# A hybrid decoder layer on one core: gate's low-rank product spread over the first projection, one warm-up matmul less, decay levels in pairs

## The chip, the cores and the metric

The kernel runs on one core of a Trainium2 chip. The metric is the device time of one execution in microseconds, from repeated executions. The profile is of one further execution; its engines are TensorE (PE, with the weight loads PEld apart), VectorE (DVE), ScalarE (ACT), GpSimd (POOL) and SyncE (SP), which issues nearly all DMAs.

## The reference

One layer on 256 tokens of width 1024, all in float32:

```python
def _hybrid_mixer(h, w_in, w_gate_up, b_gate, gla_norm_g, w_mix_o):
    proj = h @ w_in
    qa, ka, va, qg, kg, vg, rg, glr = jnp.split(proj, cuts, axis=-1)
    moba_o = _merge(_moba(_heads(qa, 8), _heads(ka, 8), _heads(va, 8)))
    log_a = jax.nn.log_sigmoid(glr @ w_gate_up + b_gate) / GLA_GATE_TEMP
    o = _gla(_heads(qg, 4), _heads(kg, 4), _heads(vg, 4), _heads(log_a, 4))
    o = o * lax.rsqrt(jnp.mean(jnp.square(o), -1, keepdims=True) + RMS_EPS) * gla_norm_g
    gla_o = _merge(o) * jax.nn.silu(rg)
    return jnp.concatenate([moba_o, gla_o], -1) @ w_mix_o

def reference(...):
    x = _layer_norm(ALPHA * x + _hybrid_mixer(x, ...), ln1_g, ln1_b)
    x = _layer_norm(ALPHA * x + _mem_xattn(x, mem, w_xq, w_xkv, w_xo), ln2_g, ln2_b)
    return _layer_norm(ALPHA * x + jnp.square(relu(x @ w_ff1)) @ w_ff2, ln3_g, ln3_b)
```

Group A is causal softmax attention (8 heads of 64), group B gated linear attention (4 heads, key width 64, value width 128, chunks of 64 tokens). Its gate comes from a low-rank product: glr has 16 columns, w_gate_up is 16x256. Within a chunk the attention of t to s is the sum over d of q[t,d] k[s,d] exp(b[t,d] - b[s,d]), with b the running sum of log_a.

## The kernel before, in words

**Precision.** A float32 operand is split into a high part (fp32r, a rounded copy made by ScalarE) and a low part (operand minus high part, by VectorE, for a few units by POOL). A projection is three products of such parts: high times high, high times low, low times high. Products of attention (scores, transposes, decay levels) run in plain float32. For the first projections the helpers `high` and `low` (L1371 and L1377 on) make it two: the high weights meet both parts of the input in one matmul of 512 columns (L1374), the low weights the high input in one of 256 (L1378).

**Weights** come in chunks of 512 columns or rows (2 MB), each in two halves of 1 MB ("units"), through a ring of four buffers, `raw`. SyncE issues a load once the low part of the unit four places earlier is made. ScalarE's `hi_half(c, half)` casts a unit into `w_hi`, VectorE's `lo_half(c, half)` subtracts into `w_lo`; both of these have two places, by the chunk's parity, so ScalarE may start on a chunk once TensorE is through with the one two before. Chunk 0 is gate queries and keys (qg, kg), 1 queries (qa), 2 keys (ka), 3 values (va), 4 and 5 values and the output gate of group B (vg, rg), 6, 7, 8, 11 the memory's keys and values, 9 and 10 the output projection.

**The first chunk** is cut finer: input and weights land alternately in eight DMAs, and `EARLY_CUTS` lists the nine pieces in which ScalarE (L564) and VectorE (L878) split them. Behind these, `w_glr` (the 16 columns of the low-rank product, 64 KB) is loaded (L378) and split into `wglr_split` (L567, L881).

**Order of work.** Every engine's order is written out by hand. PSUM has eight banks; `FRONT_FILLS` lists which product fills which bank, in order, and `begin(name)` waits until the bank's earlier content has left, `full(name)` tells that it is filled, `wait_out(name)` waits until it has been copied out. TensorE does, in this order: `WARM_UP` = 3 matmuls of 512 columns on constants (L1366; the profile shows each as two pieces); chunk 0, for each k of eight four high and four low matmuls; the low-rank product glr, 16 matmuls (L1402, L1403); half of the queries; z = glr times w_gate_up (L1426); the other half; the keys ka0 to ka3, one after another, each eight high matmuls and then eight low ones; va, scores, vg, and so on.

**Decay levels.** The attention within chunks is made in seven levels (blocks of 64, 32, ... 1) and one product across chunks (`off`). For each level VectorE makes exponents, ScalarE the exponential, POOL the products with keys and queries (L478, L488), TensorE four float32 matmuls (L1501; eight pieces in the profile), and VectorE copies what belongs to the level under a mask (`masked`, L1006). POOL's product for level n waits until TensorE has done level n - 2. The levels stand between the memory's projections xk0 to xk3, xv00, xv01, one after each half of a projection.

**DVE's order at the keys** is: low part of chunk 2's first half, z plus bias (L911), its absolute value (L916), low part of the second half (L869).

Of the kernel before, what the change touches and what calls it, by code (L numbers as in the profile page):

```python
# [21 lines left out]
S = 256  # L22
# [4 lines left out]
RANK = 16  # L27
# [11 lines left out]
WARM_UP = 3  # L39
# [71 lines left out]
def raw_count(u):  # L111
# [5 lines left out]
    [("qg0", 0), ("qg1", 1), ("kg0", 2), ("kg1", 3), ("glr", 4), ("qa0", 5), ("qa1", 6), ("qa2", 7), ("qa3", 0), ("z", 4),  # L117
     ("ka0", 1), ("ka1", 2), ("ka2", 3), ("ka3", 4), ("va0", 2)]
# [23 lines left out]
def build(nc, x, xT, memT, w_in, w_glr, w_gate_up, b_gate, gla_norm_g, w_mix_o, ln1_g, ln1_b, w_xq, w_xkv,  # L142
# [7 lines left out]
    with ctx:  # L150
# [200 lines left out]
        def _(sp):  # L351
# [176 lines left out]
        def _(act):  # L528
# [36 lines left out]
            act.wait_ge(wglr_in, 16)  # L565
            act.wait_ge(wglr_zeroed, 1)
            act.copy(wglr_parts[:, :, 0:3, 0, :], wglr_thrice).then_inc(wglr_hi, 1)  # L567
# [3 lines left out]
            hi_half(1, 0)  # L571
            right("qg0")
# [3 lines left out]
            wait_full(act, "glr")  # L576
            act.copy(glrT[:], bank[4][0:6 * RANK, 0:S]).then_inc(glr_hi, 1)
# [99 lines left out]
            memk(3)  # L677
            decay(7)
# [4 lines left out]
            hi_half(9, 0)  # L683
# [174 lines left out]
        def _(dve):  # L858
# [17 lines left out]
            for n, (u, _, a, b) in enumerate(EARLY_CUTS):  # L876
# [3 lines left out]
            dve.wait_ge(wglr_hi, 1)  # L880
            dve.tensor_tensor(wglr_parts[:, :, 0:3, 1, :], wglr_thrice, wglr_parts[:, :, 0:3, 0, :].bitcast(f32),  # L881
                              ALU.subtract).then_inc(wglr_lo, 1)
            def left(name):
# [7 lines left out]

            lo_half(1, 0)
# [6 lines left out]
            low_rows = slice(2 * RANK, 4 * RANK)  # L899
            b = wait_full(dve, "glr")  # L900
            dve.wait_ge(glr_hi, 1)
            dve.tensor_tensor(glrT[low_rows, :], b[low_rows, 0:S], glrT[low_rows, :].bitcast(f32), ALU.subtract)\
                .then_inc(freed("glr"), 1)
# [18 lines left out]
            lo_half(3, 0)  # L922
            for m in range(4):
                left(f"qa{m}")
            lo_half(3, 1)
# [116 lines left out]
            masked(0)  # L1042
            exponents(4)
            masked(1)
            lo_half(8, 0)
            exponents(5)
            masked(2)
            lo_half(8, 1)
            exponents(6)
            masked(3)  # L1050
            exponents(7)
            masked(4)
            masked(5)
            masked(6)
            lo_half(9, 0)
# [231 lines left out]
        def _(pe):  # L1287
# [93 lines left out]

            first = ["qg0", "qg1", "kg0", "kg1"]
            banks = [begin(name) for name in first]
            for k in range(8):
                unit_w, end = 1 + k // 4, 512 * (k % 4) + 512
                if k >= 2:
                    end = 1024 * (k % 4 // 2) + 1024
                if k < 2 or k % 2 == 0:
                    pe.wait_ge(early_lo, early_count(0, 512 * (k // 2) + 512))
# [9 lines left out]
            b = begin("glr")  # L1399
            pe.wait_ge(wglr_lo, 1)  # L1400
            for k in range(8):
                pe.matmul(b[:, 0:S], wglr_split[:, k, :], actA_hi[:, k, :], start=k == 0, stop=False)  # L1402
# [311 lines left out]
```

## Time and profile before

| | us |
|---|---|
| median of 3 runs | 411.12 |
| lowest, highest | 410.32, 411.77 |
| the profiled execution, its own time | 409.76 |
| its span | 407.9 |
| TensorE busy | 400.2 (98%) |
| VectorE, ScalarE, GpSimd busy | 278.1, 204.3, 63.7 |

The span is from the first to the last instruction on the core; the execution's own time has some more around it. Busy shares say which engine works most. What sets the end is told by the chain that ended last: it is followed back from the last instruction, at each step to what released it. TensorE's ends are modelled, since its matmuls are pipelined.

### The profile page before, as it was taken

What the parts mean: (1) busy time and instruction counts of PE and PEld (TensorE: products, weight loads), DVE (VectorE), ACT (ScalarE), POOL (GpSimd) and SP (SyncE); (2) the same over time, 40 slices, a digit from 0 to 9 for tenths busy, and PEclk for the clock granted to TensorE, in tenths of its full rate; (3) what the DMA queues carried; (4) which work ended last, traced back from release to release, by engine and by line L of the source; (5) the groups of instructions that cost most, each with busy time, mean ns of one, the idle gap of its engine ahead of it and who ended that gap; (6) DMA issues with size and microseconds to landing.
All of it is one profiled execution on the core that took longest, in us unless ns stands there. A gap on an engine that the chain in (4) does not pass through costs nothing.

```text
span 407.9 us, 5836 instructions
## 1 busy us (share of the span) xinstructions
PE 400.2 (98%) x2256; PEld 345.9 (85%) x2256; DVE 278.1 (68%) x357; ACT 204.3 (50%) x279; POOL 63.7 (16%) x61
## 2 busy tenths in 40 slices
PE   8999999999999999999999999999999999999993
PEld 5888888899988888999988888888888888888882
DVE  3679676998794796876658859384746475664826
ACT  5658478646354628435833457362625343545400
POOL 2089000045960105000005100000000000000000
PEclk9999999999999999999999999999999999999999
DMA  8998737635535380733554284656665727464002
GB/s 288 318 372 283 245 136 268 225 128 207 182 128 206 105 306 3 274 141 104 206 196 158 73 297 127 204 186 206 208 206 169 242 104 257 153 217 194 0 0 103
DMA packets 32220, 75.70 MB, mean 186 GB/s; under 512 B 1510, under 2 KB 3910, under 8 KB 32198
## 3 DMA queue, kind: packets, MB, share of 16 engines
q1 hardware_dynamic: 31808, 75.24, 53.4%
q10 hardware_dynamic: 390, 0.17, 0.2%
q8 instruction: 14, 0.23, 0.2%
q14 instruction: 8, 0.07, 0.0%
HBM read 74.35 MB, written 1.05 MB: 185 GB/s over the span
## 4 chain that ended last, share of the span: by engine, by line
PE 98%; DVE 1%; issue 0%; POOL 0%; DVEq 0%; POOLq 0%
PE bank L1300 21%; PE bank L1301 21%; PE bank L1302 21%; PE bank L1653 13%; PE bank L1656 7%; PE bank L1374 5%; PE bank L1378 3%; PE bank L1501 2%; PE bank L1366 1%; PE bank L1306 1%; PE bank L1453 1%; PE bank L1479 0%; PE bank L1534 0%; PE bank L1583 0%; PE bank L1445 0%; PE bank L1444 0%
## 5 line engine op out<-in xcount | busy, mean ns | idle before, releaser
L869 DVE TENSOR_TENSOR w_lo<-raw,w_hi 128x2048 fp32r<-128x2048 f32 x36 | 83.7, 2330 | 20.0 <-ACT w_hi L539 20.0
L539 ACT CAST w_hi<-raw 128x2048 fp32r<-128x2048 f32 x38 | 72.3, 1916 | 20.1 <-PE bank L1302 14.2
L1235 DVE TENSOR_TENSOR w_lo<-raw,w_hi 128x2048 fp32r<-128x2048 f32 x24 | 55.0, 2291 | 40.1 <-ACT w_hi L806 40.1
L1300 PE MATMUL bank<-w_hi,actB_hi 128*128 128x512 f32 x192 | 75.6, 394 | 0.0
L1301 PE MATMUL bank<-w_lo,actB_hi 128*128 128x512 f32 x192 | 74.8, 390 | 0.0
L1302 PE MATMUL bank<-w_hi,actB_lo 128*128 128x512 f32 x192 | 74.8, 389 | 0.0
L806 ACT CAST w_hi<-raw 128x2048 fp32r<-128x2048 f32 x24 | 46.0, 1917 | 38.2 <-PE bank L1302 38.2
L1653 PE MATMUL bank<-actA,w_hi 128*128 128x512 f32 x224 | 56.0, 392 | 0.0
L1653 PEld LDWEIGHTS bank<-actA,w_hi 128*128 128x128 f32 x224 | 40.7, 188 | 7.6
L1302 PEld LDWEIGHTS bank<-w_hi,actB_lo 128*128 128x128 f32 x192 | 36.0, 188 | 7.6
L1300 PEld LDWEIGHTS bank<-w_hi,actB_hi 128*128 128x128 f32 x192 | 36.1, 188 | 7.2
L1301 PEld LDWEIGHTS bank<-w_lo,actB_hi 128*128 128x128 f32 x192 | 36.1, 188 | 6.9
L1300 PE MATMUL bank<-w_hi,actA 128*128 128x512 f32 x96 | 38.1, 397 | 0.0
L1302 PE MATMUL bank<-w_hi,actA 128*128 128x512 f32 x96 | 37.5, 390 | 0.0
L1301 PE MATMUL bank<-w_lo,actA 128*128 128x512 f32 x96 | 37.5, 390 | 0.0
L515 POOL TENSOR_TENSOR rstd<-vareps,minus_half 128x1 f32<-128x1 f32 x6 | 3.3, 544 | 195.2 <-DVE vareps L1098 195.1
L1656 PEld LDWEIGHTS bank<-actA,w_lo 128*128 128x128 f32 x224 | 30.6, 190 | 2.2
L1656 PE MATMUL bank<-actA,w_lo 128*128 128x256 f32 x224 | 31.2, 282 | 0.0
L791 ACT COPY att<-bank 128x256 f32<-128x256 f32 x28 | 10.3, 377 | 34.7 <-PE bank L1656 34.0
L1374 PE MATMUL bank<-actA,w_hi 128*128 128x512 f32 x96 | 25.1, 400 | 0.0
L1300 PEld LDWEIGHTS bank<-w_hi,actA 128*128 128x128 f32 x96 | 18.0, 188 | 4.4 <-issue 0.7
L1302 PEld LDWEIGHTS bank<-w_hi,actA 128*128 128x128 f32 x96 | 18.0, 188 | 3.9
(188 smaller groups left out, 669.4 us busy)
## 6 DMA issues: line engine op xcount, KB each, us to landing
raw<-in_w_ff SPq DMA_DIRECT2D x32, 1024.0 KB, 5.3
raw<-in_w_in SPq DMA_DIRECT2D x10, 1024.0 KB, 7.6
raw<-in_w_xkv SPq DMA_DIRECT2D x8, 1024.0 KB, 5.0
raw<-in_w_mix_o SPq DMA_DIRECT2D x4, 1024.0 KB, 4.8
raw<-in_w_xq SPq DMA_DIRECT2D x4, 1024.0 KB, 5.2
raw<-in_w_xo SPq DMA_DIRECT2D x4, 1024.0 KB, 4.8
raw<-in_w_in SPq DMA_DIRECT2D x4, 512.0 KB, 6.0
probs<-in_ln_g SPq DMA_DIRECT2D x3, 512.0 KB, 6.2
```

Source lines behind the costliest of these rows:

```text
L539: act.copy(dst, half_view(u)).then_inc(hi_done, 1)
L791: act.copy(relu[:, f, m * S:(m + 1) * S], bank[b][:, S:2 * S]).then_inc(small_done, 1)
L806: act.copy(w_hi[:, (C_LOOP + k) % 2, half, :], raw[:, u % RAW, :]).then_inc(hi_done, 1)
L869: dve.tensor_tensor(dst, half_view(u), hi_part.bitcast(f32), ALU.subtract).then_inc(lo_done, 1)
L1235: dve.tensor_tensor(w_lo[:, c % 2, half, :], raw[:, u % RAW, :], w_hi[:, c % 2, half, :].bitcast(f32), ALU.subtract).then_inc(lo_done, 1)
L1300: pe.matmul(dst, stat[0], mov[0], start=start, stop=False, skip_group_check=on)
L1301: pe.matmul(dst, stat[0], mov[1], start=False, stop=False, skip_group_check=on)
L1302: return pe.matmul(dst, stat[1], mov[0], start=False, stop=stop, skip_group_check=on)
L1374: pe.matmul(dst[:, :].rearrange("p (h s) -> p h s", h=2), weight(c, k, m * P, (m + 1) * P)[0], actA[:, :, k, :], start=k == 0, stop=False, ...
L1378: return pe.matmul(dst[:, S:2 * S], weight(c, k, m * P, (m + 1) * P)[1], actA_hi[:, k, :], start=False, stop=k == 7, skip_group_check=True)
L1653: pe.matmul(b[:, :].rearrange("p (h s) -> p h s", h=2), w_hi[:, par, cols[k][0], cols[k][1]], actA[:, :, k, :], start=k == 0, stop=False, ...
L1656: i = pe.matmul(b[:, S:2 * S], w_lo[:, par, cols[k][0], cols[k][1]], actA_hi[:, k, :], start=False, stop=k == 7, skip_group_check=True)
```

## The change

Parts of it: one warm-up matmul less; `w_glr` loaded behind the first piece of input, and split right behind it on ScalarE and VectorE; its product in four groups, each ahead of two steps of k of chunk 0; its result copied out ahead of the queries' work on both engines; qa3 in bank 4 and z in bank 0; ka3 in bank 0 too; the second half of the values' split ahead of copying out the queries; chunk 9's first cast ahead of the last decay exponential; and levels in pairs (0, 1), (2, 3), (4, 5), and (6, off), with VectorE's masks in pairs where that fits.

```diff
-WARM_UP = 3
+WARM_UP = 2
...
-    [("qg0", 0), ("qg1", 1), ("kg0", 2), ("kg1", 3), ("glr", 4), ("qa0", 5), ("qa1", 6), ("qa2", 7), ("qa3", 0), ("z", 4),
-     ("ka0", 1), ("ka1", 2), ("ka2", 3), ("ka3", 4), ("va0", 2)]
+    [("qg0", 0), ("qg1", 1), ("kg0", 2), ("kg1", 3), ("glr", 4), ("qa0", 5), ("qa1", 6), ("qa2", 7), ("qa3", 4), ("z", 0),
+     ("ka0", 1), ("ka1", 2), ("ka2", 3), ("ka3", 0), ("va0", 2)]
...
+                if p == 0:
+                    sp.dma_start(wglr[:].rearrange("p a n -> p (a n)"), w_glr).then_inc(wglr_in, 16)
...
-            sp.dma_start(wglr[:].rearrange("p a n -> p (a n)"), w_glr).then_inc(wglr_in, 16)
...
-            for u, dma, a, b in EARLY_CUTS:
+            for n, (u, dma, a, b) in enumerate(EARLY_CUTS):
                 act.wait_ge(early_in[dma], 16)
                 act.copy(first_hi[u][:, a:b], raw[:, u, a:b]).then_inc(early_hi, 1)
+                if n == 0:
+                    act.wait_ge(wglr_in, 16)
+                    act.wait_ge(wglr_zeroed, 1)
+                    act.copy(wglr_parts[:, :, 0:3, 0, :], wglr_thrice).then_inc(wglr_hi, 1)
...
             hi_half(1, 0)
+            wait_full(act, "glr")
+            act.copy(glrT[:], bank[4][0:6 * RANK, 0:S]).then_inc(glr_hi, 1)
             right("qg0")
...
             hi_half(3, 0)
+            hi_half(3, 1)
             for m in range(4):
                 right(f"qa{m}")
-            hi_half(3, 1)
...
             memk(3)
+            hi_half(9, 0)
             decay(7)
...
+            for k in range(8):
+                if k % 2 == 0:
+                    pe.wait_ge(early_lo, early_count(0, 512 * (k // 2) + 512))
+                    for n in range(k, k + 2):
+                        pe.matmul(b[:, 0:S], wglr_split[:, n, :], actA_hi[:, n, :], start=n == 0, stop=False)
+                        i = pe.matmul(b[:, 0:S], wglr_split[:, n, :], actA_lo[:, n, :], start=False, stop=n == 7)
+                    if k == 6:
+                        i.then_inc(full("glr"), 1)
...
-            features(6, 1, B, "xk1", between=lambda: level(0))
-            level(1)
-            features(7, 0, B, "xk2", between=lambda: level(2))
-            level(3)
-            features(7, 1, B, "xk3", between=lambda: level(4))
-            level(5)
-            tokens(8, 0, B, "xv00", between={4: lambda: level(6)})
-            off()
-            tokens(8, 1, B, "xv01")
+            features(6, 1, B, "xk1", between=lambda: levels(0, 1))
+            features(7, 0, B, "xk2")
+            levels(2, 3)
+            features(7, 1, B, "xk3")
+            tokens(8, 0, B, "xv00", between={4: lambda: levels(4, 5)})
+            tokens(8, 1, B, "xv01", between={4: last_level})
```

VectorE's side (its splits of `w_glr`, glr's low part, the values' second half, and the masks) moves in the same manner.

TensorE's first rows before. L1366 is the warm-up, L1374 and L1378 the high and low products of chunk 0.

```order
1 L1366 MATMUL bank<-reset 128x512 x3
2 L1374 MATMUL bank<-actA,w_hi 128x512 x4
3 L1378 MATMUL bank<-actA,w_lo 128x256 x4
4 L1374 MATMUL bank<-actA,w_hi 128x512 x4
5 L1378 MATMUL bank<-actA,w_lo 128x256 x4
```

And now, with L1394 and L1395 the low-rank product (`again` holds its weights):

```order
1 L1369 MATMUL bank<-reset 128x512 x2
2 L1394 MATMUL bank<-actA,again 128x256
3 L1395 MATMUL bank<-actA,again 128x256
4 L1394 MATMUL bank<-actA,again 128x256
5 L1395 MATMUL bank<-actA,again 128x256
6 L1377 MATMUL bank<-actA,w_hi 128x512 x4
7 L1381 MATMUL bank<-actA,w_lo 128x256 x4
8 L1377 MATMUL bank<-actA,w_hi 128x512 x4
9 L1381 MATMUL bank<-actA,w_lo 128x256 x4
10 L1394 MATMUL bank<-actA,again 128x256
```

Four matmuls of the low-rank product now stand ahead of each two steps of k; before, all sixteen stood behind the eighth.

VectorE at the levels before, where L1006 is a level's mask, L976 and L977 the next exponents, L869 a unit's low part:

```order
108 L1006 COPY_PREDICATED att<-const,bank 128x8x64
109 L976 TENSOR_TENSOR qk<-gla 128x64x4
110 L977 TENSOR_TENSOR qk<-gla 128x64x4
111 L1006 COPY_PREDICATED att<-const,bank 128x16x32
112 L869 TENSOR_TENSOR w_lo<-raw,w_hi 128x2048
113 L976 TENSOR_TENSOR qk<-gla 128x128x2
114 L977 TENSOR_TENSOR qk<-gla 128x128x2
115 L1006 COPY_PREDICATED att<-const,bank 128x32x16
116 L869 TENSOR_TENSOR w_lo<-raw,w_hi 128x2048
```

And now:

```order
106 L1009 COPY_PREDICATED att<-const,bank 128x8x64
107 L1009 COPY_PREDICATED att<-const,bank 128x16x32
108 L979 TENSOR_TENSOR qk<-gla 128x64x4
109 L980 TENSOR_TENSOR qk<-gla 128x64x4
110 L871 TENSOR_TENSOR w_lo<-raw,w_hi 128x2048
111 L979 TENSOR_TENSOR qk<-gla 128x128x2
112 L980 TENSOR_TENSOR qk<-gla 128x128x2
113 L871 TENSOR_TENSOR w_lo<-raw,w_hi 128x2048
114 L1009 COPY_PREDICATED att<-const,bank 128x32x16
115 L1009 COPY_PREDICATED att<-const,bank 128x64x8
```

The masks of levels 1 and 3 stand right behind those of 0 and 2, and the pair (2, 3) behind a unit's low part that it stood ahead of.

## Rows read from the trace of the kernel before

**Rows 1.** Page, chain that ended last, share of the span by engine

```profile
PE 98%; DVE 1%; issue 0%; POOL 0%; DVEq 0%; POOLq 0%
```

**Rows 2.** Chain in order of time, 0 to 20 us: start us, us, what

```profile
1.49 5.42 PE bank L1366 x6
6.90 0.93 PE bank L1374 x4
...
18.12 0.11 PE bank L1402
...
19.93 3.65 PE bank L1374 x16
```

**Rows 3.** Source lines L1366, L1374 (0 to 10 us): ns min/median/max, first and last start us

```profile
L1366 PEld LDWEIGHTS bank<-reset x6: 285/337/337, 1.5 to 5.1; 128*128 128x128 f32 x6
...
L1374 PEld LDWEIGHTS bank<-actA,w_hi x11: 187/189/330, 5.9 to 9.8; 128*128 128x128 f32 x11
```

**Rows 4.** Timeline, 0 to 15 us: start us, us, engine, line, op, out<-in

```profile
5.19 1.14 ACT L564 CAST w_hi<-raw 128x512 fp32r<-128x512 f32 x2 [1.07 <-DMA raw<-in_w_in]
5.26 0.61 SPq L378 DMA_DIRECT2D wglr<-in_w_glr  x1
...
12.03 0.69 DVE L878 TENSOR_TENSOR actA<-raw,actA 128x512 fp32r<-128x512 f32 x1
...
12.91 0.51 ACT L567 CAST again<-wglr 128x384 fp32r<-128x384 f32 x1
...
14.18 0.55 DVE L881 TENSOR_TENSOR again<-wglr,again 128x384 fp32r<-128x384 f32 x1
```

**Rows 5.** DMA issues at 0.9 to 1.3 us: KB each, us to landing

```profile
raw<-in_w_in SPq DMA_DIRECT2D x1, 512.0 KB, 3.9
```

**Rows 6.** Window 5 to 10 us (last number GB/s); then SyncE's issue at 13.89 us, its landing

```profile
5.00:10.00 5.00, 5.00 (x21) 3.49 (x20) 3.11 (x5) 3.42 (x6) 0.00 (x0) 1.00 1.07 387
...
13.89 0.43 SPq L362 DMA_DIRECT2D raw<-in_w_in  x1
...
raw<-in_w_in SPq DMA_DIRECT2D x1, 1024.0 KB, 11.3
```

**Rows 7.** Timeline, 25 to 34 us, ScalarE and VectorE at the keys' weights

```profile
25.17 1.91 ACT L539 CAST w_hi<-raw 128x2048 fp32r<-128x2048 f32 x1 [3.10 <-DMA raw<-in_w_in]
...
27.11 2.29 DVE L869 TENSOR_TENSOR w_lo<-raw,w_hi 128x2048 fp32r<-128x2048 f32 x1 [1.88 <-ACT w_hi L539]
...
30.91 2.59 DVE L869 TENSOR_TENSOR w_lo<-raw,w_hi 128x2048 fp32r<-128x2048 f32 x1
```

**Rows 8.** Chain in order of time, keys (L1378), transposes (L1453), levels (L1501), behind `off`

```profile
33.15 1.15 PE bank L1378 x8
...
36.14 0.95 PE bank L1378 x8
...
68.24 1.31 PE bank L1453 x12
...
94.38 0.89 PE bank L1501 x8
...
98.14 0.89 PE bank L1501 x8
...
121.13 0.43 PE bank L1300
```

**Rows 9.** Timeline, 94 to 121 us, POOL's products for the levels

```profile
100.68 3.64 POOL L488 TENSOR_TENSOR qkdiag<-gla,qk 64x256 f32<-64x256 f32 x2
104.45 0.92 POOL L478 TENSOR_TENSOR qk<-gla,qk 128x256 f32<-128x256 f32 x1
105.44 3.63 POOL L488 TENSOR_TENSOR reset<-gla,qk 64x256 f32<-64x256 f32 x2
...
110.31 1.86 POOL L488 TENSOR_TENSOR qkdiag<-gla,qk 64x256 f32<-64x256 f32 x2
...
113.29 1.76 POOL L488 TENSOR_TENSOR reset<-gla,qk 64x256 f32<-64x256 f32 x2
```

More of the change, by code:

```diff
@@ L682, in _ @@
                 seed(bank[FILL[f"mo0{c}"][0]], 0, c)
-            hi_half(9, 0)
             evacuate("xv00", memv[:, 0, 0:512])
@@ L879, in _ @@
                     .then_inc(early_lo, 1)
-            dve.wait_ge(wglr_hi, 1)
-            dve.tensor_tensor(wglr_parts[:, :, 0:3, 1, :], wglr_thrice, wglr_parts[:, :, 0:3, 0, :].bitcast(f32),
-                              ALU.subtract).then_inc(wglr_lo, 1)
+                if n == 0:
+                    dve.wait_ge(wglr_hi, 1)
+                    dve.tensor_tensor(wglr_parts[:, :, 0:3, 1, :], wglr_thrice, wglr_parts[:, :, 0:3, 0, :].bitcast(f32),
+                                      ALU.subtract).then_inc(wglr_lo, 1)
             def left(name):
@@ L890, in left @@
                     dve.scalar_tensor_tensor(dst, b[:, 0:S], scale, dst, ALU.mult, ALU.add).then_inc(freed(name), 1)
+            low_rows = slice(2 * RANK, 4 * RANK)
+            b = wait_full(dve, "glr")
+            dve.wait_ge(glr_hi, 1)
+            dve.tensor_tensor(glrT[low_rows, :], b[low_rows, 0:S], glrT[low_rows, :].bitcast(f32), ALU.subtract)\
+                .then_inc(freed("glr"), 1)
             lo_half(1, 0)
@@ L898, in _ @@
                 .then_inc(wgu_lo, 1)
[L899 to L903, printed above, removed]
             left("qg1")
@@ L922, in _ @@
             lo_half(3, 0)
+            lo_half(3, 1)
             for m in range(4):
                 left(f"qa{m}")
-            lo_half(3, 1)
             for m in range(4):
@@ L1042, in _ @@
             masked(0)
+            masked(1)
             exponents(4)
-            masked(1)
             lo_half(8, 0)
             exponents(5)
+            lo_half(8, 1)
             masked(2)
-            lo_half(8, 1)
+            masked(3)
             exponents(6)
-            masked(3)
             exponents(7)
@@ L1053, in _ @@
             masked(5)
+            lo_half(9, 0)
             masked(6)
-            lo_half(9, 0)
             lo_half(9, 1)
@@ L1383, in _ @@
             banks = [begin(name) for name in first]
+            b = begin("glr")
+            pe.wait_ge(wglr_lo, 1)
             for k in range(8):
+                if k % 2 == 0:
[5 more added lines that the diff above has]
+                        i.then_inc(full("glr"), 1)
                 unit_w, end = 1 + k // 4, 512 * (k % 4) + 512
@@ L1388, in _ @@
                 if k < 2 or k % 2 == 0:
-                    pe.wait_ge(early_lo, early_count(0, 512 * (k // 2) + 512))
                     pe.wait_ge(early_hi, early_count(unit_w, end))
@@ L1398, in _ @@
                         i.then_inc(full(first[m]), 1)
[L1399 to L1402, printed above, removed]
-                i = pe.matmul(b[:, 0:S], wglr_split[:, k, :], actA_lo[:, k, :], start=False, stop=k == 7)
-            i.then_inc(full("glr"), 1)
             qa = [f"qa{m}" for m in range(4)]
@@ L1516, in _, with levels, last_level @@
             features(6, 0, B, "xk0")
-            features(6, 1, B, "xk1", between=lambda: level(0))
-            level(1)
-            features(7, 0, B, "xk2", between=lambda: level(2))
-            level(3)
-            features(7, 1, B, "xk3", between=lambda: level(4))
-            level(5)
-            tokens(8, 0, B, "xv00", between={4: lambda: level(6)})
-            off()
-            tokens(8, 1, B, "xv01")
+            def levels(*which):
+                for n in which:
+                    level(n)
+            def last_level():
+                level(6)
+                off()
+            features(6, 1, B, "xk1", between=lambda: levels(0, 1))
[4 more added lines that the diff above has]
+            tokens(8, 1, B, "xv01", between={4: last_level})
             for name in ("vg0", "vg1", "off0", "off1", "lv6"):
```

5 lines of the change are left out of this document (removed), and 2 rows, old and new, of the table FRONT_FILLS.

## The prediction

> **What bounds the kernel now.** I read the chain that ended last, first as its summary. TensorE has 98% of it [rows 1], so only two kinds of change can count: less work on TensorE's path, or an earlier start of it. A wait that the chain doesn't show must be looked for in the lengths of its pieces. In order of time the chain begins with the warm-up (matmuls on constants, there to raise TensorE's clock), six pieces that end at 6.91 us; the first projection starts right there, eight steps of k later the gate's low-rank product takes 1.8 us, and queries start at 19.93 [rows 2]. So before 20 us nothing waits for data: the warm-up itself holds the first projection back.
>
> The warm-up runs at the lower of TensorE's two levels, though the profile's granted clock says 1.00 there. One of its weight loads takes 337 ns, and one of the first projection's 189 [rows 3]. One piece of 512 columns takes 5.42/6 = 0.90 us [rows 2], while a decay level, float32 like the warm-up, takes 0.89 us for eight pieces of 128 columns [rows 8], 0.11 each, which makes 0.45 for 512 columns. The warm-up's piece takes twice that: 1.2 GHz against 2.4. The clock rose at about the warm-up's end.
>
> Then I looked for waits inside the chain. Later on nearly all pieces of one kind are equally long, with one exception before 50 us: the low products of ka0 (eight of 256 columns) take 1.15 us at 33.15, those of ka1 0.95 [rows 8]. These 0.20 us are a wait for the low part of the keys' second half of weights, which VectorE finishes at 30.91 + 2.59 = 33.50 [rows 7]. That chain leads back to a DMA: the keys' first half is issued in the burst that starts at 13.89, lands 11.3 us later, about 25.2 [rows 6], ScalarE starts on it at 25.17, VectorE at 27.11 [rows 7], then come two operations on z, then the half in question. None of it waits for TensorE. **This point, 33.5 us, is a gate that does not move when TensorE comes sooner.**
>
> **The change part by part.**
>
> *One warm-up matmul less.* Two pieces of 0.90 us go: 1.81 us less before the first projection, which would let it start at 5.10. But its weights aren't there: ScalarE starts on the first of them at 5.19 and takes 1.14 us for two [rows 4].
>
> *The low-rank weights ahead in SyncE's queue.* 64 KB land before the first weights instead of after them. At the 387 GB/s of 5 to 10 us [rows 6] that is 0.17 us. The issue takes 0.61 us of SyncE [rows 4], but the transfers landed 3.9 and more us after their issue [rows 5] and the engines are full, so the issue is covered; if it weren't, 0.6 us is the upper bound. I take 0.25. The Trainium skill (DMA: Bandwidth & Descriptors, Specifications) puts line rate at transfers of 512 B and up; these rows have exactly 512 B, so by it 0.17 would do. No row here shows the cost of this transfer alone.
>
> Split of these weights: ScalarE 0.51, VectorE 0.55 [rows 4]. On ScalarE it fits before the first weights land, on VectorE after the first input piece. So the product for the first two k can start at about 5.5, ahead of the first projection at about 6.1 to 6.4.
>
> *The gate's product spread.* Sixteen matmuls stay sixteen, all fp32r like their neighbours: no work less. A quarter, 0.45 us at the upper level and 0.9 at the lower, lies in the hole between warm-up and first weights; the rest, 1.36 us, stays on the path. First projection: 18.12 - 6.90 = 11.2 us [rows 2] as before. With the clock rising at the same 6.7 to 6.9, TensorE reaches the queries at about 6.35 + 0.2 (the little that is still at the lower level) + 11.2 + 1.36 = 19.1 to 19.2 instead of 19.93: **0.75 us sooner**.
>
> *Between there and the gate at 33.5.* qa3 and z swap banks: z needs qg0 freed, qa3 needs the gate's product freed, both done some us before. VectorE now waits for the gate's product (full at about 16) ahead of the queries' first half, 0.4 us more there; its result is due four us later. TensorE comes to the keys' low products 0.75 us sooner and waits 0.75 more. And the gate itself moves: VectorE ends the last input piece at 12.03 + 0.69 = 12.72 [rows 4], and only then its buffer is free and SyncE issues the queries' second half, ahead of the keys'. So what lands 0.25 later up to here makes all later landings 0.25 later. In the terms of the profiled execution the early part so ends **0.25 us worse**, its 0.75 given back in a wait of about 1.2 us.
>
> *Decay levels in pairs.* The same matmuls; four returns to fp32r fewer. What a return costs comes out of two rows: eight such pieces and a return take 0.89, twelve of the probabilities' transposes and a return 1.31 [rows 8]. So a piece is 0.42/4 = 0.105, a return 0.05, four of them **0.2 us gained**. The lower bound is 0; the upper is the return behind the chunks' product, where the next piece takes 0.43 [rows 8] instead of the 0.93/4 = 0.23 of its kind [rows 2]: 0.8 for four. I take 0.2, from the levels' own row. A pair waits for its second level. A stretch between levels is 98.14 - 94.38 - 0.89 = 2.87 us [rows 8]. Levels 2 and 3 so come at 94.38 + 1.78 + 3 x 2.87 = 104.8 and 105.7; POOL has level 3 ready at 104.32 [rows 9]. Level 4's products on POOL may start only when level 2 has left (105.7 instead of 104.45), take 4.6, level 5's some 3, ready at 113.3; TensorE is there at 115.0. Level 6 (2.75 on POOL, once level 4 has left at 115.9) and the chunks' product 1.4 more are ready at 120.1, wanted at 122.3. The second of a pair is wanted another 0.9 later, so the slacks are 1.4, 2.6 and 3.1 us: no wait.
>
> *The last pieces.* The queries' and values' splits swapped with evacuations, and chunk 9's low half later (about 128.5, wanted about 130.4): nothing.
>
> **Sum.** 0.25 - 0.2 = 0.05 us worse, for the profiled execution (409.76 us, span 407.9). But the three runs shown lie 0.56 to 2.01 us above it, median 1.36. The likeliest place for such a spread is the start: the clock that rises once, at a moment of its own, in work at half speed. A run in which it rises later reaches the gate later than 33.5, and there a sooner TensorE does count: half of the 1.3 us by which it starts real work sooner (5.5 instead of 6.9, less the transfer), 0.65 us, and the 0.25 costs nothing; with the pairs 0.85. So the bounds are +0.05 and -0.85. I take -0.35, between them because nothing in the profile shows where the 1.36 lie: 411.12 - 0.35 = **410.8 us**. That is within 0.3% (1.2 us), about what a measurement of this kernel can tell from no change. The forecast's own range is 410.3 to 411.4.
>
> The Trainium skill (TensorE: Matmul & The Clock Gate, Part 1) says that the engine starts throttled and that sustained activity releases it. The weight loads above agree. By this rule taking work out ahead of the release speaks against the change; that is the third rival.
>
> **The rivals.**
>
> 1. *The warm-up's 1.81 us are kept in full* and the pairs give their 0.2, less the 0.17 of the transfer: 411.12 - 1.84 = 409.3. For it: in runs with a late clock the gate at 33.5 is no bound, and if the clock rises after an amount of work at the same place in the program the whole goes. Against it: weights aren't there before 5.2, and the profiled execution has 0.2 us of room. Chance 0.22.
>
> 2. *The levels wait:* level 3 late, since POOL took 3.64 us for a part that took 1.86 in another level [rows 9]. If levels 2 and 3 each took 1.2 us longer there, level 3 would be 2.4 late against a slack of 1.4: 1.0 us of waiting, 410.8 + 1.0 = 411.8. Still within 0.3%. Chance 0.05.
>
> 3. *Slower: the clock rises later.* Place: TensorE's first microseconds. With a warm-up of 3.6 us and a hole of some 0.4 us behind it, TensorE may be kept at 1.2 GHz for longer. It took 5.4 us from first matmul to the rise now. Another 5.4 would cost half, 2.7 us; the wait at the keys covers 1.2 of it: 411.12 + 0.05 + 1.5 = 412.7. It decides from a rise at about 6.9 + 2.4 = 9.3 us, from where the cover is used up. Against it: the engine is busy most of the time all the same. Chance 0.12.
>
> **How the numbers follow.** Forecast 0.61, rivals 0.22, 0.05 and 0.12. Faster by over 0.3%: 0.22, from the first. Within: 0.66. Slower: 0.12. The range takes in the first rival's value at its edge, 409.3, and the low part of the third, up to 412.0.
>
> **What would show it.** In the new profile four warm-up pieces; the first projection at about 6.3; the queries at about 19.1; the low products of ka0 some 1.2 us longer than those of ka1, ended by VectorE at about 33.7; from there on the chain with the old distances; at the levels pairs of about 1.73 us. Wrong, if ka0's wait is no longer than 0.2 us and queries start before 18.5, or if weight loads of over 300 ns reach behind 9 us.

## The result, and the profile after

| us | before | changed |
|---|---|---|
| median (lowest to highest) | 410.79 (409.47 to 412.3), 18 runs | 411.62 (410.91 to 413.11), 18 runs |
| the profiled execution, its own time | 409.76 | 410.91 |
| its span | 407.9 | 409.1 |

The ratio is 1.0025, with an interval of 1.0014 to 1.0035: the change costs about 1.0 us (the medians stand 0.83 apart). The forecast was a gain of 0.35 us. The two profiled executions stand apart by 1.15 us. They lie 1.03 and 0.71 us below the medians of their kernels, the changed one is the fastest of its 18 runs, so what their traces show side by side is two good executions and not the typical ones. Lines from about L375 on have moved, by six up to the levels and by up to eleven behind them; L1377 and L1381 are now the high and low products that were L1374 and L1378, L1303 to L1305 the product va that was L1300 to L1302.

The page's chain that ended last, the share by engine:

```profile
PE 89%; DMA 4%; DVE 3%; issue 1%; SPq 1%; ACT 1%; DVEq 0%
```

TensorE had 98% of it before [rows 1]. The chain now starts with DMAs, so something ahead of the later work waits for data. Where it waits can be seen in the groups of instructions of the first 50 us (the last field is the idle time just before them, and what ended it):

```profile
L1377 PE MATMUL bank<-actA,w_hi 128*128 128x512 f32 x96 | 24.5, 394 | 0.7 <-ACT w_hi L565 0.7
...
L1381 PE MATMUL bank<-actA,w_lo 128*128 128x256 f32 x96 | 13.9, 283 | 0.6 <-DVE w_lo L871 0.6
...
L1303 PE MATMUL bank<-w_hi,actA 128*128 128x512 f32 x8 | 3.2, 404 | 0.5 <-DVE qk L891 0.5
...
L1394 PE MATMUL bank<-actA,again 128*128 128x256 f32 x8 | 2.1, 290 | 0.4 <-DVE again L884 0.4
```

Four waits of TensorE: for the first weights, for the low part of the keys' second half (the keys' gate), at va0 for copies that VectorE makes out of PSUM (L891), and for the weights of the low-rank product. The waits for the first weights and for the low-rank product's come before the keys' gate, and the chain that ended last doesn't pass through them. Here it is in order of time (start us, us, what):

```profile
3.75 6.55 DMA raw<-in_w_in
...
14.22 11.10 DMA raw<-in_w_in
...
25.34 1.93 ACT w_hi L540
...
31.32 2.52 DVE w_lo L871
...
33.88 0.74 PE bank L1381 x4
34.62 1.86 PE bank L1377 x8
36.48 0.95 PE bank L1381 x8
...
39.26 0.97 PE bank L1381 x8
...
43.48 0.50 PE bank L1303
...
49.22 0.43 PE bank L1450 x4
```

The keys' gate has moved from 33.50 [rows 7] to 33.84, and TensorE goes on the moment it opens. Half of that is the landing: ScalarE starts on the keys' weights at 25.34 instead of 25.17. The other half is VectorE, whose split of the first half takes 2.44 us instead of 2.29; the kernel before with two warm-ups has 2.40 there too, so this part need not come from the load. The low products of ka0 end at 34.62, 0.32 us after the 34.30 of [rows 8], and ka1's begin at 36.48 instead of 36.14. Those of ka2, at 39.26, keep that distance. Then va0 begins 0.8 us late, the 0.34 of the gate included, and its first piece takes 0.50 instead of 0.23. The first score product (L1444 before, L1450 now) starts at 49.22 instead of 48.14. The two rows of before, va0's first piece and the score:

```profile
42.68 0.23 PE bank L1300
...
48.14 0.43 PE bank L1444 x4
```

That is **1.08 us: 0.33 from the keys' gate, 0.75 from va0**. Hardly anything is added behind that: the spans differ by 1.15 us, 0.07 more. The three pairs of levels and the last level by itself stand in the same chain:

```profile
95.46 1.78 PE bank L1507 x16
...
105.88 1.78 PE bank L1507 x16
...
116.16 1.78 PE bank L1507 x16
...
123.42 0.89 PE bank L1507 x8
```

A pair takes 1.78, twice the 0.89 of one level [rows 8]. Three stretches lie between two pairs, 105.88 - 95.46 - 1.78 = 8.64 us, 2.88 each, with one return to fp32r in the three; before, with a return in each, one took 2.87. So a return costs nothing that these rows show. Nothing was saved, and no level waited.

What made the landings later is in the timeline of the first microseconds (start us, us, engine, line, operation, idle time before it):

```profile
0.75 0.43 SPq L374 DMA_DIRECT2D raw<-in_xT  x1
1.24 0.46 SPq L377 DMA_DIRECT2D wglr<-in_w_glr  x1
1.75 0.43 SPq L378 DMA_DIRECT2D raw<-in_w_in  x1
...
5.37 0.38 PE L1394 MATMUL bank<-actA,again 128*128 128x256 f32 x1 [0.38 <-DVE again L884]
...
6.11 1.14 ACT L565 CAST w_hi<-raw 128x512 fp32r<-128x512 f32 x2 [1.58 <-DMA raw<-in_w_in]
```

The first weights reach ScalarE at 6.11 instead of 5.19 [rows 4]. 0.51 us of that is the issue: the weights' DMA stands at 1.75, where the low-rank weights' own issue, at 1.24, has taken its place. The rest is in the transfers. Windows of one microsecond (the last number is GB/s, the one ahead of it the DMA engines' share), 2 to 5 us, before and then the changed kernel:

```profile
2.00:3.00 1.00, 1.00 (x2) 0.34 (x1) 0.00 (x0) 0.22 (x2) 0.77 (x1) 1.00 0.93 254
3.00:4.00 1.00, 1.00 (x2) 0.34 (x1) 0.00 (x0) 0.50 (x1) 0.00 (x0) 1.00 1.02 317
4.00:5.00 1.00, 1.00 (x2) 0.34 (x1) 0.69 (x1) 0.12 (x1) 0.00 (x0) 1.00 1.02 327
```

```profile
2.00:3.00 1.00, 1.00 (x2) 0.34 (x1) 0.00 (x0) 0.22 (x2) 0.78 (x1) 1.00 0.86 278
3.00:4.00 1.00, 1.00 (x2) 0.34 (x1) 0.00 (x0) 0.50 (x1) 0.00 (x0) 1.00 0.62 122
4.00:5.00 1.00, 0.98 (x2) 0.00 (x0) 0.85 (x2) 0.53 (x2) 0.00 (x0) 1.00 0.95 305
```

Between 3 and 4 us, where the low-rank weights land (issued at 1.24, landed 2.4 us later), the rate stands at 122 GB/s instead of 317. The missing 195 KB are 0.5 us of transfer at 387 GB/s [rows 6].

### The profile page after: what moved, and what is told of

Same layout as the page of the kernel before. It is cut to its first block, busy times and chain, and to the rows that moved or that the text cites. A ratio compares the mean times of both kernels' runs of the same rounds, so it can differ in the third digit from the quotient of the medians.

```text
span 409.1 us, 5834 instructions
## 1 busy us (share of the span) xinstructions
PE 399.2 (98%) x2254; PEld 345.3 (84%) x2254; DVE 276.1 (68%) x357; ACT 204.2 (50%) x279; POOL 64.3 (16%) x61
## 4 chain that ended last, share of the span: by engine, by line
PE 89%; DMA 4%; DVE 3%; issue 1%; SPq 1%; ACT 1%; DVEq 0%
PE bank L1303 21%; PE bank L1305 21%; PE bank L1304 21%; PE bank L1664 13%; PE bank L1667 7%; DMA raw<-in_w_in 4%; PE bank L1507 2%; PE bank L1309 1%; PE bank L1377 1%; PE bank L1381 1%; PE bank L1459 1%; DVE w_lo L871 1%; DVE qk L891 1%; PE bank L1485 0%; ACT w_hi L540 0%
## 5 line engine op out<-in xcount | busy, mean ns | idle before, releaser
L1303 PE MATMUL bank<-w_hi,actB_hi 128*128 128x512 f32 x192 | 75.6, 394 | 0.0
L1305 PE MATMUL bank<-w_hi,actB_lo 128*128 128x512 f32 x192 | 74.8, 389 | 0.0
L1305 PEld LDWEIGHTS bank<-w_hi,actB_lo 128*128 128x128 f32 x192 | 36.0, 188 | 7.6
L1303 PEld LDWEIGHTS bank<-w_hi,actB_hi 128*128 128x128 f32 x192 | 36.1, 188 | 7.2
L1303 PE MATMUL bank<-w_hi,actA 128*128 128x512 f32 x96 | 38.3, 399 | 0.5 <-DVE qk L891 0.5
L1305 PE MATMUL bank<-w_hi,actA 128*128 128x512 f32 x96 | 37.5, 391 | 0.0
L1377 PE MATMUL bank<-actA,w_hi 128*128 128x512 f32 x96 | 24.5, 394 | 0.7 <-ACT w_hi L565 0.7
L1303 PEld LDWEIGHTS bank<-w_hi,actA 128*128 128x128 f32 x96 | 18.0, 188 | 5.1 <-DVE qk L891 0.7
L1305 PEld LDWEIGHTS bank<-w_hi,actA 128*128 128x128 f32 x96 | 18.0, 188 | 3.9
```

What stands on the lines that cost most here:

```text
L1303: pe.matmul(dst, stat[0], mov[0], start=start, stop=False, skip_group_check=on)
L1305: return pe.matmul(dst, stat[1], mov[0], start=False, stop=stop, skip_group_check=on)
L1377: pe.matmul(dst[:, :].rearrange("p (h s) -> p h s", h=2), weight(c, k, m * P, (m + 1) * P)[0], actA[:, :, k, :], start=k == 0, stop=False, ...
```

## The experiments

My theory after the result: the low-rank weights ahead on SyncE's queue make all landings later, so the keys' gate opens later, and the values' second half in VectorE's order adds a wait at va0. The rivals: the pairs cost something; the clock rises later with one warm-up matmul less; the early start of TensorE is worth something and is only hidden.

**The values' second half put back behind the queries' copies** (in the changed kernel; the same on VectorE).

```diff
             hi_half(3, 0)
-            hi_half(3, 1)
             for m in range(4):
                 right(f"qa{m}")
+            hi_half(3, 1)
```

> The changed kernel with one part undone: the second half of the values' weights is again split after the queries have been copied out of their banks, on ScalarE and VectorE. Theory (two waits): the changed kernel loses 0.3 us at the keys' low products and 0.7 us at va0, where TensorE waits for VectorE to copy ka1 out of its bank. Without the second, va0 starts at about 43.0 instead of 43.48 and the span is 408.3 to 408.5, so 0.3 to 0.6 us over the kernel before instead of 1.0. Rival (early start): the loss is made before 34 us by the low-rank weights' transfer and this edit changes nothing, span 409.1. Rival (clock): the shorter warm-up costs it, again no change.

Measured: 411.48 us (410.92 to 412.07), ratio to before 1.0026 (1.0012 to 1.0039). The wait at va0 is gone, but in its profile the keys' weights reach ScalarE at 26.11, and the chain shows the gate 0.8 us later than in the changed kernel:

```profile
34.69 0.74 PE bank L1381 x4
...
49.28 0.43 PE bank L1450 x4
```

The first score starts at the same place, 49.28. In this execution a gate 1.15 us later than the 33.50 of before cost as much as gate and va0 together in the changed kernel's. So the two waits, which lie one behind the other, can hide each other. The order of VectorE alone doesn't explain the loss.

**The pairs alone** (in the kernel before: the levels' order on TensorE, VectorE and ScalarE, and xv01 ahead of lv6 in the banks, as in the change).

```diff
-            features(6, 1, B, "xk1", between=lambda: level(0))
-            level(1)
-            features(7, 0, B, "xk2", between=lambda: level(2))
-            level(3)
...
+            features(6, 1, B, "xk1", between=lambda: levels(0, 1))
+            features(7, 0, B, "xk2")
+            levels(2, 3)
```

> The kernel before with the levels in pairs alone (with their masks, bank order and chunk 9's cast). Theory: two levels together take 1.78 us, twice 0.89, in the changed kernel's chain, so a pair saves nothing: 0.0 +- 0.1 us, span 407.9. Rival (the forecast's term): 0.2 us faster. Rival (POOL): level 6 is ready only 1.3 us ahead of its place, so in some runs TensorE waits and it is slower by 0.3 or more.

Measured: 410.31 us, ratio 0.9999 (0.9986 to 1.0012). The pairs are worth nothing that can be measured, in either direction.

**One warm-up matmul less, alone** (in the kernel before).

```diff
-WARM_UP = 3
+WARM_UP = 2
```

> The kernel before with two warm-up matmuls instead of three, nothing else. Theory (gate at the keys): the first projection starts about 1 us sooner, near 5.9 us, and all of it is given back as a wait in the low products of ka0, which end at 34.3 as before: 0.0 +- 0.1 us. Rival (late clock in other runs): up to 0.65 us faster in the median, since runs with a late clock come to the keys later than the gate. Rival (clock kept low): slower by 0.5 us or more, with weight loads of over 300 ns beyond 7 us.

Measured: 410.48 us, ratio 0.9997 (0.9984 to 1.001). In its profile the first projection starts at 6.16 and the span is 407.3, 0.6 less than before: the keys' weights came at 24.06 in that execution, and no gate was met. That is the fastest of its twelve runs (409.1 to 411.35): the earlier start is real there, and what becomes of it in the others isn't shown.

**The keys' low parts first** (in the kernel before: on VectorE the keys' second half ahead of z, the values' first half ahead of the last operations on z; on ScalarE the values' first half ahead of the exponential and logarithm).

```diff
             lo_half(2, 0)
+            lo_half(2, 1)
             dve.wait_ge(small_in, 32)
...
-            lo_half(2, 1)
+            lo_half(3, 0)
             dve.wait_ge(softplus_done, 1)
```

> The kernel before with the keys' second half and the values' first half of weights split ahead of the two stretches of work on z (VectorE and ScalarE), nothing else. Theory: the gate at 33.5 us moves to about 32.3, the 0.2 us wait in ka0's low products goes, and 0.2 us are gained (span 407.7), no more, since the warm-up now bounds the early part. Rival: the work on z comes late and z's bank or the queries' copies make TensorE wait at ka3 or va0: slower by some tenths.

Measured: 410.1 us, ratio 0.9994 (0.998 to 1.0008). The keys' wait is gone and a new one stands at va0, in the page's groups:

```profile
L1300 PE MATMUL bank<-w_hi,actA 128*128 128x512 f32 x96 | 38.3, 399 | 1.2 <-DVE qk L888 1.2
```

z went behind the keys, the queries' and keys' copies behind z, and va0's bank is one that ka1 has to leave. In this execution one gate opened and the next one held. It is one of the four slower runs (411.08); eight of the twelve lie at 409.7 to 410.25, and whether they waited at va0 isn't shown.

**The load alone** (in the kernel before: only the low-rank weights' DMA moved ahead on SyncE's queue, as in the change; three warm-ups, the product behind the projection).

```diff
+                if p == 0:
+                    sp.dma_start(wglr[:].rearrange("p a n -> p (a n)"), w_glr).then_inc(wglr_in, 16)
...
-            sp.dma_start(wglr[:].rearrange("p a n -> p (a n)"), w_glr).then_inc(wglr_in, 16)
```

> The kernel before with the load of the low-rank weights moved ahead of the first weights on SyncE's queue, as in the change, and nothing else. Theory (transfer): this one transfer of 64 KB is the cost. The first weights reach ScalarE at 6.1 to 6.8 us instead of 5.2 to 5.6, the keys' weights 0.2 to 0.9 later than 25.2, and the median is 0.2% (0.6 to 1.0 us) slower, as in the changed kernel. Rival (bytes alone, 64 KB at 387 GB/s): first weights 0.2 later, time within 0.05%. Rival (the product's place among the projections costs): no change here.

Measured: 411.15 us (410.37 to 412.16), ratio 1.0016 (1.0 to 1.0031), span 410.3. The first weights come to ScalarE at 7.19, the keys' at 26.43, and the keys' gate opens at 32.49 + 2.59 = 35.08, 1.58 us later than before. TensorE waits for the first weights (1.4 us), at the keys' low products (0.2) and at va0 (0.5). The first and the last of these in the page's groups:

```profile
L1301 PE MATMUL bank<-w_hi,actA 128*128 128x512 f32 x96 | 38.3, 399 | 0.5 <-DVE qk L889 0.5
...
L1375 PE MATMUL bank<-actA,w_hi 128*128 128x512 f32 x96 | 24.4, 393 | 1.4 <-ACT w_hi L565 1.4
```

The window from 3 to 4 us has 103 GB/s. The profiled execution is the slowest of the twelve (412.16 us), so these waits are more than the typical ones. With nothing else changed, the load makes 0.65 us of the 1.0 by its ratio, though its interval reaches from no loss to all of it.

**The same load on ScalarE's queue** (in the changed kernel).

```diff
-                if p == 0:
-                    sp.dma_start(wglr[:].rearrange("p a n -> p (a n)"), w_glr).then_inc(wglr_in, 16)
...
+            act.dma_start(wglr[:].rearrange("p a n -> p (a n)"), w_glr).then_inc(wglr_in, 16)
             act.wait_ge(half_done, 1)
```

> The changed kernel with the same load issued on ScalarE's queue at its start, so that it takes no issue slot of SyncE. If the cost is SyncE's issue slot (0.5 us), the first weights come back to about 5.4 us and the time to 0.1% of the kernel before. If it is the transfer itself (128 rows of 512 B in front of the first weights), they stay at 6 us or later and the time stays 0.2 to 0.3% above it.

Measured: 410.69 us (409.54 to 411.12), ratio 0.9999 (0.9984 to 1.0014). The loss is gone. The same 64 KB land early, but SyncE's first issues stand where they stood before, and there is no hole:

```profile
0.74 0.45 ACTq L558 DMA_DIRECT2D wglr<-in_w_glr  x1
...
1.24 0.46 SPq L376 DMA_DIRECT2D raw<-in_w_in  x1
...
5.64 1.14 ACT L564 CAST w_hi<-raw 128x512 fp32r<-128x512 f32 x2 [0.76 <-DMA raw<-in_w_in]
```

```profile
3.00:4.00 1.00, 1.00 (x2) 0.34 (x1) 0.00 (x0) 0.15 (x1) 0.00 (x0) 1.00 1.07 380
```

So it isn't the bytes ahead of the weights; it is the place in SyncE's queue. And since every other part of the change is still in this kernel, all of them together cost or gain no more than its interval, 0.16%. In this profile the keys' gate opens at 33.53, but va0's wait brings the first score to 49.16, as in the changed kernel: its profiled execution (410.84 us) is no better than that one (410.91), while the median is, by 0.9 us. In this execution VectorE's order costs 1 us at va0 with the landings on time; over all runs no loss is left that can be measured.

**Both gates opened, two warm-ups** (in the kernel before: keys first as above, and the copies of ka0 and ka1 ahead of the values' second half).

```diff
-WARM_UP = 3
+WARM_UP = 2
...
                 left(f"qa{m}")
+            left("ka0")
+            left("ka1")
             lo_half(3, 1)
-            for m in range(4):
-                left(f"ka{m}")
+            left("ka2")
+            left("ka3")
```

> The kernel before with two warm-up matmuls, the keys' weights split ahead of the work on z, and ka0 and ka1 copied out ahead of the values' second half. Theory: VectorE's queue between 25 and 43 us is the bound of the early part, at two places (keys' low products, va0). With both moved, TensorE is free and the earlier start shows: span 407.1 to 407.3 where the first projection starts at 6.2 instead of 6.9, median 0.2 to 0.3% faster than the kernel before. Rival (something else varies between runs, behind 43 us): no faster than two warm-ups alone (0.9997).

Measured: 410.95 us, ratio 1.0 (0.9982 to 1.0017). Both waits are gone (the keys' gate opens at 29.78 + 2.29 = 32.07), and nothing is gained. The chain of its profile shows why:

```profile
6.01 2.04 PE bank L1376 x4
8.05 0.85 PE bank L1380 x4
8.91 1.71 PE bank L1376 x4
10.61 0.75 PE bank L1380 x4
```

A matmul of 512 columns takes 0.43 to 0.51 us until about 11, twice the 0.23 of before [rows 2]: TensorE stayed at 1.2 GHz for four microseconds longer. The twelve runs fall into two groups, three of 409.0 to 409.65 and nine of 410.55 to 411.31.

**The low-rank product one group later** (in the changed kernel: its weights behind the first weights, their split behind the third piece, the product in groups of 8, 4 and 4 ahead of k = 2, 4, 6).

```diff
-                if n == 0:
+                if n == 2:
                     act.wait_ge(wglr_in, 16)
...
-                    for n in range(k, k + 2):
+                    if k == 2:
+                        pe.wait_ge(wglr_lo, 1)
+                    for n in range(0 if k == 2 else k, k + 2 if k else 0):
```

> The changed kernel with the low-rank weights loaded behind the first two steps' weights instead of ahead of them, split behind these, and the product in three groups ahead of the steps 2, 4 and 6 of k (eight, four, four matmuls). Theory (transfer): the first weights are back at 5.4 us; of the loss 0.6 us or more goes, the time is within 0.1% of the kernel before. Rival (spreading costs, for its place in VectorE's or TensorE's queue): it stays at 1.002 or more.

Measured: 410.99 us (410.1 to 413.52), ratio 1.0014 (0.9996 to 1.0032). On time itself this is inconclusive: the profile has the late clock too, and the interval takes in most of the answers. But the first weights are back at 5.47 us, and the window from 3 to 4 us has 297 GB/s. Third on SyncE's queue, behind the first weights, the same load makes no hole.

**Both gates opened, three warm-ups and one warm-up** (the kernel of two experiments back, with WARM_UP = 3 and 1).

```diff
-WARM_UP = 2
+WARM_UP = 3
```

> e7 with three warm-up matmuls again (the kernel before with only VectorE's order at the keys mended). In e7's profile TensorE stayed at the lower level until about 11 us (first high products 0.43 to 0.51 us each) and its twelve runs fall in two groups, three at 409.0 to 409.7 and nine at 410.5 to 411.3. Theory (clock after the warm-up): with three warm-ups the clock is up at the warm-up's end in more of the runs, the lower group holds half or more of them, median 409.8 to 410.2, ratio 0.998. Rival (the groups have nothing to do with the warm-up): the same split, median near 410.9. In the profile, if the clock rises early: first projection at 6.9 or sooner, no wait at ka0 or va0, span 407.6 to 407.8.

> e7 with one warm-up matmul. Theory (clock after the warm-up): TensorE idles from 3.2 to 6 us, the clock comes late in nearly all runs, the first projection's first steps run at 1.2 GHz and the times lie in one group at 410.5 to 411.5; profile: high products at 0.43 us or more each until 8 us or later. Rival (the clock's moment doesn't depend on the warm-up): the same two groups as e7, a quarter of the runs below 409.7.

Measured with three: **409.59 us (409.04 to 409.97), ratio 0.9976 (0.9966 to 0.9986)**, one group of runs, no wait at the keys or at va0. With one: 411.44 us (410.5 to 412.12), ratio 1.002 (1.0008 to 1.0032); in its profile the first projection runs at half speed to about 11. In order, the start of both chains:

```profile
1.49 5.49 PE bank L1368 x6
6.97 0.99 PE bank L1376 x4
```

```profile
6.37 2.05 PE bank L1376 x4
8.42 0.85 PE bank L1380 x4
9.27 1.71 PE bank L1376 x4
```

Against the early group of the two-warm-up kernel (its median 409.41) the third warm-up costs 0.2 us; against the late group (median 411.12) it spares 1.5.

**The change with all of it mended** (the load on ScalarE's queue, the values' second half back, keys first, ka0's and ka1's copies first; two warm-ups).

```diff
             hi_half(2, 1)
+            hi_half(3, 0)
             act.wait_ge(zabs_done, 1)
...
-            hi_half(3, 0)
-            hi_half(3, 1)
             for m in range(4):
                 right(f"qa{m}")
+            hi_half(3, 1)
```

> The changed kernel with everything mended that cost something so far: the low-rank weights loaded by ScalarE's queue, the values' second half behind the queries' copies, keys' weights split ahead of the work on z, ka0 and ka1 copied out ahead of the values' second half. Theory: no wait at the keys and none at va0; with the clock up early TensorE reaches va0 at about 41.9 (6.2 for the first projection, 0.45 of the low-rank product in the hole), span 407.0, the best of all; with a late clock 408.5 to 409. Median 409.5 to 410.5, ratio 0.997 to 0.999. Rival (clock): the median is that of e7, 410.9, since the hole behind two warm-ups leaves the clock down.

Measured: 409.14 us (408.76 to 411.19), ratio 0.9983 (0.9967 to 1.0). Its span of 407.1 is the shortest of all, the first score starts at 47.26, but five of twelve runs lie at 410.54 to 411.19, seven at 408.76 to 409.25: two groups, 2.0 us apart by their medians (410.87 and 408.91).

**The kernel before once more.**

> The kernel before once more, for its profile and for the spread of its runs. Theory: ratio 1.0 +- 0.001; its runs lie between 409.4 and 412 again. Its profile shows one of two things: keys' weights at 25.2 and a short wait at ka0, or a late clock (pieces of 0.43 us and more behind the warm-up) with va0 at 44 or later and a span of 409 or more.

Measured: 409.98 us, ratio 0.999 (0.9978 to 1.0003), and the keys' wait again. In its profile and in that of the pairs alone the gate opens at 33.64 (31.05 + 2.59) and 33.61, against 33.50 in the profile that the prediction read. The clock's moment differs too. The last weight load of this warm-up took 192 ns and not 337, so TensorE was at the upper level before the warm-up ended, at 1.49 + 4.50 = 5.99 instead of 6.91, and the first projection waited for its weights:

```profile
1.49 4.50 PE L1366 MATMUL bank<-reset 128*128 128x512 f32 x6 [1.49 <-POOL reset L442]
6.17 1.17 PE L1374 MATMUL bank<-actA,w_hi 128*128 128x512 f32 x4 [0.19 <-ACT w_hi L564]
```

The 0.7 us of earlier start are gone at the keys' gate, and the span is 408.1 against 407.9. That is what the prediction said of an earlier start, seen in the kernel before itself.

**The change, and the mended change, with three warm-ups.**

> The changed kernel with three warm-up matmuls again. If part of the changed kernel's 0.25% comes from runs in which the clock rises late after the shorter warm-up, this brings it back: median 411.2 or below, ratio 1.001. If all of it comes from the transfer ahead of the first weights and the waits behind it (VectorE at the keys and va0, which hide TensorE's own pace), nothing changes: ratio 1.002 to 1.003, waits of 0.6 to 1 us again at the keys' low products or at va0.

> e11 with three warm-up matmuls. e11's runs fall in two groups, seven at 408.8 to 409.3 and five at 410.5 to 411.2. If the second group are runs with a late clock after the shorter warm-up, it goes or shrinks to one or two of twelve, and the first group moves up by the 0.5 us or more by which three warm-ups hold the first projection back: all near 409.2 to 409.9, as in e9. If the groups have another cause, five of twelve stay at 410.5 or more.

Measured: the change 412.01 us (410.88 to 412.42), ratio 1.0033 (1.002 to 1.0047), span 410.2, with the first weights at 6.84, the keys' at 26.09 and both waits. Adding the warm-up back doesn't mend the change. The mended change: **409.39 us (408.95 to 409.93), ratio 0.9974 (0.9964 to 0.9985)**, in one group. The upper group of the version with two warm-ups is gone, as the late clock would have it. Against the kernel without the spread product, 0.9976, it isn't told apart: with the gates open the spreading itself is worth nothing that these runs can show.

## Why the prediction was wrong

**The transfer term, 0.25 us with an upper bound of 0.6, was mis-sized.** The prediction took the issue as covered, since transfers landed 3.9 and more us after it. It wasn't: the weights' own issue moved from 1.24 to 1.75, and their landing with it. In the four profiles with the load ahead on SyncE's queue the first weights reach ScalarE at 6.11 to 7.19, in the twelve others at 5.19 to 5.64; the keys' weights at 25.34 to 26.43, in the others at 24.06 to 25.76. So where 0.25 was said, the first weights came 0.9 to 2.0 us later than the 5.19 of before, and the load alone cost 0.65 us. The changed kernel's own profile is the mildest of the four, with the gate 0.33 us late, and its 25.34 is only 0.03 behind the 25.31 of the second profile of before; its copy with the values' half put back and the one with three warm-ups have the gate 1.1 to 1.2 late, the load alone 1.6. The Trainium skill (DMA: Bandwidth & Descriptors, Specifications) puts line rate at transfers of 512 B and up. The same rows of 512 B came with 103 to 124 GB/s around them second on SyncE's queue, in four profiles, and with 380 to 385 from ScalarE's queue, in three. So the size of the rows didn't decide, and the rule didn't tell this case's cost. Why the rate is low in that place isn't shown.

**"The last pieces: nothing" failed.** The values' second half ahead of the queries' copies makes va0 wait 0.5 to 0.8 us, in the changed kernel, in the one with the load on ScalarE's queue and in the one with three warm-ups; with the old order it stood at 0.5 in the run with the load alone, where the keys' weights came latest, at 26.43. In the two profiles read side by side this is the larger miss: of the 1.15 us, 0.75 stand here against nothing forecast, 0.33 at the gate against 0.25. Undone alone it brought nothing; the keys' gate of that profile was 1.15 us late by itself. The prediction had followed TensorE to its first wait and stopped there; VectorE is one long chain from the keys' low parts through z, the values and the copies, and TensorE meets it twice.

**The step from 411.12 to 410.8 failed.** The −0.35 put the spread of the runs down to a late clock that the change would shorten. Eight profiles have three warm-ups, two of them of the kernel before itself. In them the clock's moment does differ (the warm-up of before ended at 6.91 in one and at 5.99 in the other), but in none does it lie behind 7.5 us. What the spread of its runs is, isn't shown directly. It is gone in both kernels with open gates and three warm-ups (409.04 to 409.97 and 408.95 to 409.93, where before has 409.09 to 411.46 beside the second), which fits landings that vary from run to run and stop TensorE only where the gates are tight. The landings do vary: the eight profiles with SyncE's loads in the old order have the keys' weights at 24.06 to 25.33. But the two of the kernel before itself, at 25.17 and 25.31, are both of faster runs (409.76 and 409.9), so what its runs of 411 us do is open. Without this step the forecast would have been +0.05, still 1.0 us too low; the two terms above and the pairs' 0.2 make up that.

**The pairs' 0.2 us are 0.** The row of the transposes that gave "a return 0.05" wasn't a comparable piece; 1.78 is 2 x 0.89, and stretches with one return in three are as long as those with one in each. Of the levels' slacks the prediction was right: none waited.

**Right: the early gain is swallowed at VectorE's gate.** TensorE reached the queries 0.3 us sooner (19.47 against 19.77 in the timeline), not 0.75, since the first weights were late. The rest was lost at the keys' low products, ended by VectorE at 33.84, where 33.7 was said; the wait was 0.6 us, where 1.2 was said. The first rival, all of it kept, didn't come.

**The third rival** gave the right sign for another reason. The late clock exists: three profiles with two or one warm-ups have it, and the upper of the two groups of runs lies 1.7 to 2.0 us above the lower one; that the upper one is the late clock rests on one profile from each kind of group, and on its absence with three warm-ups. But the changed kernel's profile doesn't have it: its low-rank products already take 0.11 a piece from about 5.6 on. And with the third warm-up put back the loss stays. How often it comes in the changed kernel isn't shown; its runs don't fall into two groups. The Trainium skill (TensorE: Matmul & The Clock Gate, Part 1: The HAM clock gate) says that sustained activity releases the throttle. The runs agree in direction: one warm-up had it late, two in some profiles, three in none.

**What is left open.** That the load's place makes the loss is shown by taking it away (ratio 0.9999 instead of 1.0025). How much of it the gate passes on and how much VectorE's order adds isn't: the load alone gave 0.65 us and the whole change 1.0, with intervals that overlap, and the two waits hide each other. The swaps of banks and the place of chunk 9's cast were never undone by themselves in the changed kernel.

## What to carry to other kernels

At the start of a kernel the order and number of issues on a queue is a cost by itself: put a small early load on an idle engine's queue, or behind the first data that the work waits for. When a gain is swallowed at a gate, open that gate, then read the trace again for the next one: the keys' low parts first gave nothing alone, nothing with the copies and a trimmed warm-up, and 1.0 us (ratio 0.9976) with the copies and the full warm-up. Before trimming a warm-up, look at several executions: one profile with the early clock says little of the others. The same holds for any profile: ask where its own time stands among the runs before reading a cost from it.

## What the runs showed of the hardware

- With a 64 KB load in 128 rows of 512 B second on SyncE's queue, the DMA engines moved 103 to 124 GB/s in the microsecond where it lands, and the transfer queued behind it was late (first weights at 6.11 to 7.19 in four profiles, 5.19 to 5.64 in twelve). From ScalarE's queue there was no hole: 380 to 385 GB/s in three profiles. Nor was there with the load third on SyncE's queue: 297 in one.
- TensorE's clock had risen by about 7.5 us in thirteen of sixteen profiles, and rose at about 11 us in three; in none between. Nothing in the granted clock shows it: the row says 1.00 while pieces of 512 columns take 0.43 to 0.51 us instead of 0.23, in the kernel with both gates open and two warm-ups:

```profile
8.00:11.00 3.00, 3.00 (x12) 2.61 (x11) 1.92 (x3) 2.46 (x4) 0.00 (x0) 1.00 1.08 379
```

- Going between float32 and fp32r products cost nothing that can be measured (0.89 and 1.78 us for one and two levels, a stretch of 2.87 with a return in each, of 2.88 with one in three).
